# One weight load for two neighbouring ring slots, instead of one load each, in a one-core diffusion trunk

## The chip, the core and the metric

The kernel runs on one core of a Trainium2 chip. The metric is device time in microseconds (us); lower is better. A core has TensorE (PE; its weight loads are shown as PEld), VectorE (DVE), ScalarE (ACT), GpSimd (POOL) and SyncE (SP). SP and POOL each issue DMAs on a queue of their own, and both queues run on the same 16 DMA engines.

## The reference, cut to what matters

Two layers over 256 latent tokens of width 2048; layer 0 also reads 256 context tokens. All is float32. Layer 0 mixes tokens by differential attention, layer 1 by a gated short convolution, and each is followed by a gated ConvFFN of inner width 5632:

```python
for i in range(DEPTH):                        # 2 layers
    sh1, sc1, g1, sh2, sc2, g2 = adaln(c, w_ada[i], b_ada[i])   # silu(c) @ w_ada + b_ada
    hl = modulate(rmsnorm(xl), sh1, sc1)
    if i % 2 == 0: yl, _ = diff_attn_mixer(hl, hc, w_qkv, w_o, ...)   # K and V of the context too
    else:          yl = short_conv_mixer(hl, w_in, conv_w, w_out)     # (gb * conv3(gc * xv)) @ w_out
    xl = xl + g1 * yl
    xl = xl + g2 * conv_ffn(modulate(rmsnorm(xl), sh2, sc2), w_up[i], conv_w[i], w_down[i])
return rmsnorm(xl, final_gain)
```

The large products are `h @ w` with w of qkv 2048x6144, o 2048x2048, in 2048x6144, out 2048x2048, and twice up 2048x11264 and down 5632x2048.

## The kernel before

**Units and phases.** All weights but those of `w_ada` come through a ring of four slots. A *unit* is what one slot holds: 4 tiles of 128 rows by 256 columns of a weight, 512 KB (`KU = 4`, `SLAB = 256`, `RING = 4`). A *slab* is 256 output columns; it takes four units, one in each slot, and in the down phases twelve, of which the last four hold 3 tiles (384 KB). There are 800 units in this order: V (32 units of another shape), K, Q and O (32 each), up0 (176), dn0 (96), sin (96, the product with `w_in`), so (32), up1 (176), dn1 (96). Unit n sits in slot n mod 4; `4 * quad + slot` in the code is n.

**Three rings, one behind the other.** Each unit passes through `raw` (float32, filled by DMA), `w_hi` (ACT's rounded copy) and `w_lo` (DVE's difference raw - w_hi), each with four slots:

- SP, `load` (the DMA is L376): waits until DVE has made `w_lo` of unit n-4, which frees the raw slot, and issues the DMA of unit n.
- ACT, `hi` (L591): waits for the DMA (`raw_full[slot]`) and until PE has used unit n-4 (`w_used`), and copies.
- DVE, `lo` (L1070): waits for `hi` of the unit, and subtracts.
- PE, `unit` (L1770 and L1772): waits for `lo` of the unit, and issues for each tile and each half of the slab a matmul of 512 columns with `w_hi` (high and low halves of the activations) and one of 256 columns with `w_lo`. In K the same is done for the context too (L1760, L1761). V has lines of its own (L1687 to L1689), and its DMA is L385.

**Order of the work.** Every engine's order is written out by hand. ACT and DVE begin each unit with its `hi` or `lo` and then do, in that order, what is due at this point: the slab before is copied from PSUM (L634, L1210), convolved, gated or added to the residual, and DVE multiplies chunks of `w_ada` by the condition (L1131, and L1187 for broad chunks), which gives the modulation vectors. These chunks are loaded by POOL's queue into rings of their own (`ada_ring`, two slots of 512 KB; `broad_ring`, two of 1 MB). PE takes up the next slab but one only when the slab's PSUM banks have been read (`acc_read`).

**Between phases** that begin with a norm, PE waits for the sum of squares of the last slab and for the modulated activations.

In the O phase the first eight units (`O_FIRST`) are taken from two slabs in turn, between parts of the attention.

Of the kernel before, what the change touches and what calls it, by code (L numbers as in the profile page):

```python
# [7 lines left out]
ACT = mybir.ActivationFunctionType  # L8
# [8 lines left out]
QK = 2048  # L17
D_FF = 5632
# [6 lines left out]
SLAB = 256  # L25
RING = 4
KU = 4
# [10 lines left out]
V_UNITS = 32  # L38
UNITS, SLABS = {}, {}
# [73 lines left out]
def down_tiles(k):  # L113

    return (4 * k, 4) if k < 8 else (32 + 3 * (k - 8), 3)


def program(nc, x, c, ctx_in, c_ctx, w_ada, b_ada, w_qkv, w_o, lq1, lk1, lq2, lk2, subln, w_in, conv_in,
            w_out, w_up, conv_ffn, w_down, final_gain, ident_in, rope_cos_in, rope_sin_in, out):
    tiles = lambda w: w.rearrange("(t p) n -> p t n", p=P)  # L120
    qkv_w, o_w, in_w, out_w = tiles(w_qkv[0]), tiles(w_o[0]), tiles(w_in[0]), tiles(w_out[0])
# [6 lines left out]
    with ExitStack() as scope:  # L128
# [13 lines left out]
        def at(name, shape, dt, offset):  # L142
            return nc.alloc_sbuf_tensor_at(name, shape, dt, offset=offset)
# [15 lines left out]
        res = at("res", [P, KT, T], F32, at_res)  # L159

        raw = at("raw", [P, RING, KU, SLAB], F32, at_raw)
        w_hi = at("w_hi", [P, RING, KU, SLAB], F32R, at_hi)
        w_lo = at("w_lo", [P, RING, KU, SLAB], F32R, at_lo)

# [56 lines left out]
        def first_chunk(b, q):  # L221

            if b == 0:
                return first_c[:, q + 2, :, :] if q in (4, 5) else first_x[:, q, :, :]
            return first_x[:, 4 + q, :, :] if q < 2 else first_c[:, q - 2, :, :]

        def sums_slot(n):
            return first_x[:, 6 + n % 4, :, :] if n % 4 < 2 else first_c[:, 4 + n % 4, :, :]
# [47 lines left out]
        raw_full = [sem(f"raw_full{n}") for n in range(RING)]  # L276
        hi_made, lo_made, w_used = sem("hi_made"), sem("lo_made"), sem("w_used")
# [29 lines left out]
        def wait(eng, s, n):  # L307

            if isinstance(n, int) and n <= 0:
                return  # L310
            eng.wait_ge(s, n)
# [40 lines left out]
        @block.sync  # L352
        def _(sp):


            def ada_rows(q, col):
                return ada_w[0][:, 2 * q:2 * q + 2, col:col + ADA_COLS]

            def to_multiply(n):

                g, q = n // 8 + 1, n % 8

                wait(sp, start_used, n - 3)
                sp.dma_start(start_ring[:, n % 4, :, :], ada_rows(q, SH1 * P + g * ADA_COLS)).then_inc(start_full[n % 4], 16)

            def to_sum(n):

                g, q = n // 8 + 1, n % 8

                sp.wait_ge(start_step, 32 if n < 4 else 32 + 4 * (n - 3))  # L370
                sp.dma_start(sums_slot(n), ada_rows(q, SC1 * P + g * ADA_COLS)).then_inc(sums_full[n % 4], 16)

            def load(quad, slot, w, tile, n_tiles, col):

                wait(sp, lo_made, 4 * quad + slot - 3)
                sp.dma_start(raw[:, slot, 0:n_tiles, :], w[:, tile:tile + n_tiles, bass.ds(col, SLAB)]  # L376
                             ).then_inc(raw_full[slot], 16)

            wide = raw[:, :, :, :].rearrange("p r (t h) n -> p r t (h n)", h=2)

            def v_unit(n):
                g, slab, k = n // 8, n % 8 // 2, n % 2

                wait(sp, lo_made, n - 3)
                sp.dma_start(wide[:, n % 4, :, :], qkv_w[:, 4 * g + 2 * k:4 * g + 2 * k + 2, slab * VSLAB + 2 * QK:(slab + 1) * VSLAB + 2 * QK]  # L385
                             ).then_inc(raw_full[n % 4], 16)

            for q in range(8):
                for b, col in enumerate((SC1, SH1)):
                    sp.dma_start(first_chunk(b, q), ada_rows(q, col * P)).then_inc(first_full[8 * b + q], 16)  # L390
                if q == 0:
                    sp.dma_start(x_tok[:, :, :], x_rows).then_inc(x_loaded, 16)
                if q == 2:
                    sp.dma_start(ctx_tok[:, :, :], ctx_rows).then_inc(ctx_loaded, 16)
                if q == 5:
                    v_unit(0)
            for n in range(1, 4):
                v_unit(n)
            for n in range(24):
                to_sum(n)  # L400
                to_multiply(n)
                v_unit(n + 4)
            for n in range(28, V_UNITS):
                v_unit(n)
            with sp.Fori(0, 8) as s:
                for k in range(4):
                    load(s + UNITS["k"] // 4, k, qkv_w, 4 * k, 4, s * SLAB + QK)

            def plain(phase, w, base):
                with sp.Fori(0, 8) as s:  # L410
                    for k in range(4):
                        load(s + UNITS[phase] // 4, k, w, 4 * k, 4, s * SLAB + base)

            def up(phase, w):
                with sp.Fori(0, FT // 2) as j:
                    for h in range(2):
                        for k in range(4):
                            load(2 * j + (UNITS[phase] // 4 + h), k, w, 4 * k, 4, j * SLAB + h * D_FF)

            def down(phase, w):  # L420
                with sp.Fori(0, 8) as s:
                    for k in range(12):
                        tile, n = down_tiles(k)
                        load(3 * s + (UNITS[phase] // 4 + k // 4), k % 4, w, tile, n, s * SLAB)

            plain("q", qkv_w, 0)
            for n, (s, k) in enumerate(O_FIRST):
                load(UNITS["o"] // 4 + n // 4, n % 4, o_w, 4 * k, 4, s * SLAB)
            with sp.Fori(2, 8) as s:
                for k in range(4):  # L430
                    load(s + UNITS["o"] // 4, k, o_w, 4 * k, 4, s * SLAB)
            up("up0", up_w[0])
            down("dn0", dn_w[0])

            with sp.Fori(1, 9) as n:
                for h, first in ((0, D), (1, 2 * D), (2, 0)):
                    for k in range(4):
                        load(3 * n + (UNITS["sin"] // 4 + h - 3), k, in_w, 4 * k, 4, n * SLAB + (first - SLAB))
            plain("so", out_w, 0)
            up("up1", up_w[1])  # L440
            down("dn1", dn_w[1])

            for t in range(2):
                sp.wait_ge(fin_scaled[t], 1)
                sp.dma_start(out_rows[:, t, :], out_tok[:, t, :]).then_inc(fin_stored, 16)
            sp.wait_ge(fin_stored, 32)
# [90 lines left out]
        def _(se):  # L537
# [47 lines left out]

            def hi(quad, slot, n_tiles=KU):

                se.wait_ge(raw_full[slot], 16 * quad + 16)

                wait(se, w_used, 4 * quad + slot - 3)  # L590
                nc.scalar.activation(w_hi[:, slot, 0:n_tiles, :], raw[:, slot, 0:n_tiles, :], ACT.Copy).then_inc(hi_made, 1)  # L591

            keep_tokens(0, xn_l, xn_kept)
            keep_tokens(1, xn_c, ctx_kept)
            copy_rows(0)
            hi(0, 0)
            modulate(0, 0)
            hi(0, 1)
            modulate(0, 1)
            se.wait_ge(vecs_turned, 1)  # L600
# [9 lines left out]
            for g in range(4):  # L610
                for u in range(8):
                    n = 8 * g + u
                    if n + 2 < V_UNITS:
                        hi((n + 2) // 4, (n + 2) % 4)
                    if 2 <= n < 10:
                        keep_v(n - 2)
                    if u == 6 and g < 3:
                        copy_rows(g + 1)
                    if n == 3:
                        se.wait_ge(lam_summed, 1)  # L620
                        nc.scalar.activation(lam_exp[:, :], ps[:, 7, 16:18], ACT.Exp).then_inc(lam_exped, 1)
                    if u == 7 and g < 3:
                        if g == 1:
                            se.wait_ge(ada_reduced, ADA_WIDE[0])
                        modulate(g + 1, 0)
                        modulate(g + 1, 1)
# [354 lines left out]
        def _(ve):  # L981
# [85 lines left out]
            def lo(quad, slot, n_tiles=KU):  # L1067

                ve.wait_ge(hi_made, 4 * quad + (slot + 1))
                nc.vector.tensor_tensor(w_lo[:, slot, 0:n_tiles, :], raw[:, slot, 0:n_tiles, :],  # L1070
                                        w_hi[:, slot, 0:n_tiles, :], ALU.subtract).then_inc(lo_made, 1)

            def add_mods(g):
# [16 lines left out]
            ve.wait_ge(plus_one, 2)  # L1090
            add_mods(0)
            lo(0, 0)
            low_h(0, 0)
            lo(0, 1)
            low_h(0, 1)

# [42 lines left out]
            for g in range(4):  # L1139
                for u in range(8):  # L1140
                    n = 8 * g + u
# [953 lines left out]
```

## Time and profile before

| | |
|---|---|
| Time, three runs | 2691.7 us median (2685.12 to 2699.36) |
| Profiled execution | 2694.76 us, its span 2693.1 us |
| PE busy | 2603.8 us, 97% of the span |
| DVE, ACT, POOL busy | 2002.1, 1290.7, 198.5 us |
| Mean granted TensorE clock | 0.981 |
| DMA | 623.51 MB, mean 232 GB/s; SP's queue 50.8% and POOL's 19.9% of the 16 engines' span |

PE is busy for nearly all of the span, and the chain that ended last runs through PE for 90% of it. The other engines have idle time on average, but DVE has little of it from up0 to so. A DMA's time to landing is counted from its issue to the last of its semaphore's updates.

### The profile page before, as it was taken

The numbers are of one execution on the slowest core, as the hardware profiler recorded it, in microseconds if no ns is written. First come the engines' busy times: TensorE is split into PE (matmuls) and PEld (weight loads), VectorE is DVE, ScalarE is ACT, GpSimd is POOL, SyncE is SP. The second block draws the span as 40 slices with busy tenths as digits, with TensorE's granted clock in tenths as the row PEclk, the third lists the DMA queues.
The fourth block names the chain that finished last, engine by engine and source line by source line (L and its number), as shares of the span: only waits on it lengthen the run. The fifth ranks groups of instructions, "written<-read, shape, count | busy, mean of one in ns | idle before, by whom it ended". The sixth has DMA issues, their size and how long they took to land.

```text
span 2693.1 us, 39832 instructions
## 1 busy us (share of the span) xinstructions
PE 2603.8 (97%) x14306; PEld 2196.5 (82%) x14306; DVE 2002.1 (74%) x2571; ACT 1290.7 (48%) x1730; POOL 198.5 (7%) x301
## 2 busy tenths in 40 slices
PE   6999999998989999999999899999899999999998
PEld 3666788876878888888888788888788888888887
DVE  5776988676778887997778678978788876665543
ACT  4322233467655554555444444445555545554443
POOL 1000222000000000110111001101000000000000
PEclk8999999999999999999999899999999999999999
DMA  8765988333657786886999679978678865565553
GB/s 309 267 238 166 303 280 275 116 106 129 204 179 250 261 264 217 284 288 210 288 296 296 224 253 319 340 229 274 201 243 271 264 185 186 184 186 186 182 183 129
DMA packets 464924, 623.51 MB, mean 232 GB/s; under 512 B 18772, under 2 KB 404214, under 8 KB 457616
## 3 DMA queue, kind: packets, MB, share of 16 engines
q1 hardware_dynamic: 424256, 450.94, 50.8%
q0 software_dynamic: 40208, 170.51, 19.9%
q8 instruction: 95, 1.56, 0.2%
q14 instruction: 45, 0.37, 0.0%
q10 hardware_dynamic: 320, 0.13, 0.0%
HBM read 619.41 MB, written 2.10 MB: 231 GB/s over the span
## 4 chain that ended last, share of the span: by engine, by line
PE 90%; DVE 4%; ACT 3%; issue 3%; DMA 1%; SPq 0%; ACTq 0%; POOL 0%; DVEq 0%
PE ps L1770 48%; PE ps L1772 24%; PE ps L1760 4%; PE ps L1761 2%; PE ps L1631 2%; PE ps L1687 2%; PE ps L1688 2%; PE ps L1689 2%; PE ps L1699 1%; DMA first_c<-in_w_ada_dram 1%; ACT w_hi L591 1%; DVE w_lo L1070 1%; ACT rot L640 1%; DVE s_max L1350 0%; PE ps L1706 0%
## 5 line engine op out<-in xcount | busy, mean ns | idle before, releaser
L1770 PE MATMUL ps<-xs,w_hi 128*128 128x512 f32 x3840 | 1364.6, 400 | 21.8 <-issue 21.8
L1070 DVE TENSOR_TENSOR w_lo<-raw,w_hi 128x1024 fp32r<-128x1024 f32 (+1 forms) x800 | 957.6, 1201 | 383.7 <-ACT w_hi L591 382.4
L591 ACT ACTIVATE w_hi<-raw 128x1024 fp32r<-128x1024 f32 (+1 forms) x800 | 831.7, 1041 | 856.0 <-PE ps L1772 555.8
L1772 PE MATMUL ps<-xs,w_lo 128*128 128x256 f32 x3840 | 1077.1, 280 | 0.0
L1770 PEld LDWEIGHTS ps<-xs,w_hi 128*128 128x128 f32 x3840 | 726.4, 189 | 199.3 <-issue 26.1
L1772 PEld LDWEIGHTS ps<-xs,w_lo 128*128 128x128 f32 x3840 | 729.3, 190 | 3.3 <-issue 3.1
L1770 PE MATMUL ps<-act,w_hi 128*128 128x512 f32 x1408 | 494.6, 397 | 0.0
L1772 PE MATMUL ps<-act,w_lo 128*128 128x256 f32 x1408 | 392.8, 279 | 0.0
L1770 PEld LDWEIGHTS ps<-act,w_hi 128*128 128x128 f32 x1408 | 264.3, 188 | 63.1
L1772 PEld LDWEIGHTS ps<-act,w_lo 128*128 128x128 f32 x1408 | 265.2, 188 | 0.0
L634 ACT ACTIVATE y<-ps 128x512 f32<-128x512 f32 x128 | 76.7, 599 | 206.7 <-PE ps L1772 206.7
L1210 DVE TENSOR_TENSOR y<-y,ps 128x512 f32<-128x512 f32 x128 | 87.9, 687 | 99.1 <-ACT y L634 99.0
L502 POOL DMA_DIRECT2D ada_ring<-in_w_ada_dram x128 | 91.2, 713 | 783.9 <-DVE ada_sum L1131 557.9
L1131 DVE SCALAR_TENSOR_TENSOR ada_sum<-ada_ring,cond,ada_sum 128x512 f32<-128x512 f32 x185 | 138.7, 750 | 8.1 <-DMA ada_ring<-in_w_ada_dram 4.0
L1187 DVE SCALAR_TENSOR_TENSOR broad_sum<-broad_ring,cond,broad_sum 128x2048 f32<-128x2048 f32 x45 | 105.6, 2346 | 0.0
L1770 PE MATMUL ps<-heads_out,w_hi 128*128 128x512 f32 x256 | 93.6, 409 | 1.0 <-DVE y L1210 0.8
L1760 PE MATMUL ps<-cs,w_hi 128*128 128x512 f32 x256 | 91.8, 399 | 2.0 <-DVE v_rows L1105 2.0
L1760 PE MATMUL ps<-xs,w_hi 128*128 128x512 f32 x256 | 91.1, 397 | 1.8 <-DVE v_rows L1105 1.8
L1770 PE MATMUL ps<-z,w_hi 128*128 128x512 f32 x256 | 89.8, 396 | 0.0
L1772 PE MATMUL ps<-heads_out,w_lo 128*128 128x256 f32 x256 | 72.0, 281 | 0.0
L1761 PE MATMUL ps<-cs,w_lo 128*128 128x256 f32 x256 | 71.6, 280 | 0.0
L1772 PE MATMUL ps<-z,w_lo 128*128 128x256 f32 x256 | 71.3, 279 | 0.0
(219 smaller groups left out, 2609.6 us busy)
## 6 DMA issues: line engine op xcount, KB each, us to landing
raw<-in_ffn_w_up_dram SPq DMA_DIRECT2D x352, 512.0 KB, 4.4
ada_ring<-in_w_ada_dram POOLq DMA_DIRECT2D x168, 512.0 KB, 5.5
raw<-in_ffn_w_down_dram SPq DMA_DIRECT2D x128, 512.0 KB, 3.4
raw<-in_attn_w_qkv_dram SPq DMA_DIRECT2D x96, 512.0 KB, 5.5
broad_ring<-in_w_ada_dram POOLq DMA_DIRECT2D x48, 1024.0 KB, 6.2
raw<-in_sconv_w_in_dram SPq DMA_DIRECT2D x96, 512.0 KB, 6.0
raw<-in_ffn_w_down_dram SPq DMA_DIRECT2D x64, 384.0 KB, 3.1
ada_ring_kv<-in_w_ada_dram POOLq DMA_DIRECT2D x40, 512.0 KB, 6.2
```

Of the source, the lines that this page charges most:

```text
L502: pool.dma_start(ada_slot(q % ADA_SLOTS), ada_w[layer][:, 2 * q:2 * q + 2, col:col + ADA_COLS]).then_inc(ada_full[q % ADA_SLOTS], 16)
L591: nc.scalar.activation(w_hi[:, slot, 0:n_tiles, :], raw[:, slot, 0:n_tiles, :], ACT.Copy).then_inc(hi_made, 1)
L634: nc.scalar.activation(dst, ps[:, bank:bank + 2, 0:T], ACT.Copy).then_inc(a_copied, 1)
L1070: nc.vector.tensor_tensor(w_lo[:, slot, 0:n_tiles, :], raw[:, slot, 0:n_tiles, :], w_hi[:, slot, 0:n_tiles, :], ALU.subtract).then_inc(lo_ ...
L1131: nc.vector.scalar_tensor_tensor(out=out, in0=w, scalar=scalar, in1=out, op0=ALU.mult, op1=ALU.add).then_inc(ada_step, 1)
L1187: nc.vector.scalar_tensor_tensor(out=broad_sum[:, :], in0=w, scalar=scalar, in1=broad_sum[:, :], op0=ALU.mult, op1=ALU.add).then_inc(broad ...
L1210: nc.vector.tensor_tensor(dst, dst, ps[:, bank:bank + 2, T:2 * T], ALU.add).then_inc(acc_read, 1)
L1631: last = mm(ps[0:2, 6, :], cond[:, :, 2 * q + t], rows[:, t, :], start=(q == 0 and t == 0), stop=(q == 7 and t == 1))
L1760: mm(ps[:, bank + m, :], w_hi[:, k, t, cols], src[:, 4 * k + t, :], start=(k == 0 and t == 0), stop=False)
L1761: last = mm(ps[:, bank + m, 0:T], w_lo[:, k, t, cols], src[:, 4 * k + t, 0:T], start=False, stop=(k == 3 and t == 3))
L1770: mm(ps[:, bank + m, :], w_hi[:, slot, t, cols], src[:, tile + t, :], start=(is_first and t == 0), stop=False)
L1772: last = mm(ps[:, bank + m, 0:T], w_lo[:, slot, t, cols], src[:, tile + t, 0:T], start=False, stop=(is_last and t == n_tiles - 1))
```

## The change

From K on, one DMA brings the weights of two units into two neighbouring slots: 8 tiles, 1 MB; in the down phases 6 tiles, 768 KB, for two units of 3 tiles. `load_two` waits for `lo_made >= 4 * quad + slot - 2`, that is until DVE has made `w_lo` of both units that were in the two slots, and signals the even slot's semaphore alone. ACT waits for the DMA only before the even unit; for the odd unit it then needs none, except in V and in the eight units of `O_FIRST`, which still come one by one. The second of two short units now lies right behind the three tiles of the first, and `raw_unit` gives both engines the place. `hi`, `lo` and PE's work stay one per unit, and their order is unchanged.

```diff
+        raw_tiles = raw[:, :, :, :].rearrange("p r t n -> p (r t) n")
+        raw_unit = lambda slot, n: raw_tiles[:, KU * (slot // 2 * 2) + n * (slot % 2):KU * (slot // 2 * 2) + n * (slot % 2) + n, :]
...
+            def load_two(quad, slot, w, tile, n_tiles, col):
+
+                wait(sp, lo_made, 4 * quad + slot - 2)
+                sp.dma_start(raw_tiles[:, KU * slot:KU * slot + 2 * n_tiles, :], w[:, tile:tile + 2 * n_tiles, bass.ds(col, SLAB)]
+                             ).then_inc(raw_full[slot], 16)
...
                 with sp.Fori(0, 8) as s:
-                    for k in range(4):
-                        load(s + UNITS[phase] // 4, k, w, 4 * k, 4, s * SLAB + base)
+                    for k in (0, 2):
+                        load_two(s + UNITS[phase] // 4, k, w, 4 * k, 4, s * SLAB + base)
...
-                    for k in range(12):
+                    for k in range(0, 12, 2):
                         tile, n = down_tiles(k)
-                        load(3 * s + (UNITS[phase] // 4 + k // 4), k % 4, w, tile, n, s * SLAB)
+                        load_two(3 * s + (UNITS[phase] // 4 + k // 4), k % 4, w, tile, n, s * SLAB)
...
             def hi(quad, slot, n_tiles=KU):
 
-                se.wait_ge(raw_full[slot], 16 * quad + 16)
+                single = V_UNITS // 4
+                if slot % 2 == 0 or isinstance(quad, int) and quad < single:
+                    se.wait_ge(raw_full[slot], 16 * quad + 16)
+                elif isinstance(quad, int) and 0 <= quad - UNITS["o"] // 4 < 2:
+                    se.wait_ge(raw_full[slot], 16 * (single + quad - UNITS["o"] // 4) + 16)
 
                 wait(se, w_used, 4 * quad + slot - 3)
-                nc.scalar.activation(w_hi[:, slot, 0:n_tiles, :], raw[:, slot, 0:n_tiles, :], ACT.Copy).then_inc(hi_made, 1)
+                nc.scalar.activation(w_hi[:, slot, 0:n_tiles, :], raw_unit(slot, n_tiles), ACT.Copy).then_inc(hi_made, 1)
...
             def lo(quad, slot, n_tiles=KU):
 
                 ve.wait_ge(hi_made, 4 * quad + (slot + 1))
-                nc.vector.tensor_tensor(w_lo[:, slot, 0:n_tiles, :], raw[:, slot, 0:n_tiles, :],
+                nc.vector.tensor_tensor(w_lo[:, slot, 0:n_tiles, :], raw_unit(slot, n_tiles),
                                         w_hi[:, slot, 0:n_tiles, :], ALU.subtract).then_inc(lo_made, 1)
```

The loops of K, O from its third slab on, up and sin are changed in the same way as `plain` above.

## Rows read from the trace of the kernel before

**Rows 1.** The page: engines' busy time, and the chain that ended last.
```profile
PE 2603.8 (97%) x14306; PEld 2196.5 (82%) x14306; DVE 2002.1 (74%) x2571; ACT 1290.7 (48%) x1730; POOL 198.5 (7%) x301
...
PE 90%; DVE 4%; ACT 3%; issue 3%; DMA 1%; SPq 0%; ACTq 0%; POOL 0%; DVEq 0%
```

**Rows 2.** Waits of PE from 300 us on: us in total, times, longest.
```profile
PE ps L1770 <- issue: 21.8, 3, 8.0
PE ps L1825 <- DVE o_rows L1372: 8.3, 5, 2.8
PE ps L1783 <- ACT part_c L669: 7.1, 3, 2.7
...
PE ps L1770 <- DVE w_lo L1070: 0.2, 1, 0.2
```

**Rows 3.** Windows by phase: K, up0's second part, dn0, up1's second part, dn1.
```profile
core 0: us, PE busy (x) PEld busy (x) DVE busy (x) ACT busy (x) POOL busy (x), PEclk, DMA share, GB/s
...
271.00:500.00 229.00, 225.18 (x1276) 195.88 (x1275) 191.20 (x254) 70.40 (x88) 52.08 (x74) 0.99 0.80 264
...
1000.00:1265.00 265.00, 265.00 (x1530) 232.35 (x1529) 225.15 (x301) 139.00 (x183) 24.77 (x35) 0.99 0.80 253
1265.00:1515.00 250.00, 250.00 (x1459) 219.14 (x1458) 194.39 (x240) 112.39 (x133) 32.80 (x46) 1.00 0.89 282
...
2145.00:2409.00 264.00, 264.00 (x1504) 229.51 (x1503) 184.95 (x234) 140.03 (x184) 0.53 (x1) 0.99 0.61 188
2409.00:2670.00 261.00, 261.00 (x1489) 226.78 (x1488) 133.02 (x141) 118.20 (x143) 0.00 (x0) 1.00 0.55 177
```

**Rows 4.** Windows inside sin: all work, then work on w_lo alone.
```profile
1591.00:1772.00 181.00, 181.00 (x1041) 158.35 (x1040) 163.58 (x176) 83.47 (x96) 22.37 (x34) 1.00 0.94 320
...
1591.00:1772.00 181.00, 143.46 (x513) 96.64 (x512) 77.19 (x64) 1.00 0.94 320
```

**Rows 5.** Groups of instructions on the whole span (the page): hi and lo.
```profile
L1070 DVE TENSOR_TENSOR w_lo<-raw,w_hi 128x1024 fp32r<-128x1024 f32 (+1 forms) x800 | 957.6, 1201 | 383.7 <-ACT w_hi L591 382.4
L591 ACT ACTIVATE w_hi<-raw 128x1024 fp32r<-128x1024 f32 (+1 forms) x800 | 831.7, 1041 | 856.0 <-PE ps L1772 555.8
```

**Rows 6.** Tile raw in 1599 to 1602 us: issues, first and last start, landing.
```profile
L1070 DVE TENSOR_TENSOR w_lo<-raw,w_hi x3: 1221/1221/1225, 1597.8 to 1600.2; 128x1024 fp32r<-128x1024 f32 x3
...
L376 SPq DMA_DIRECT2D raw<-in_sconv_w_in_dram x3: 373/373/373, 1599.2 to 1601.6; - x3
...
DMA to landing us min/median/max: 6.1/6.3/6.4
```

**Rows 7.** DMA issues by window: up0 first part, up0 second, dn0, sin, up1, dn1.
```profile
raw<-in_ffn_w_up_dram SPq DMA_DIRECT2D x85, 512.0 KB, 4.6
broad_ring<-in_w_ada_dram POOLq DMA_DIRECT2D x15, 1024.0 KB, 5.5
...
raw<-in_ffn_w_up_dram SPq DMA_DIRECT2D x91, 512.0 KB, 4.7
...
raw<-in_ffn_w_down_dram SPq DMA_DIRECT2D x64, 512.0 KB, 5.2
ada_ring<-in_w_ada_dram POOLq DMA_DIRECT2D x46, 512.0 KB, 5.4
...
raw<-in_sconv_w_in_dram SPq DMA_DIRECT2D x96, 512.0 KB, 6.0
broad_ring<-in_w_ada_dram POOLq DMA_DIRECT2D x16, 1024.0 KB, 7.2
...
raw<-in_ffn_w_up_dram SPq DMA_DIRECT2D x176, 512.0 KB, 3.8
...
raw<-in_ffn_w_down_dram SPq DMA_DIRECT2D x64, 512.0 KB, 3.3
raw<-in_ffn_w_down_dram SPq DMA_DIRECT2D x32, 384.0 KB, 2.9
```

**Rows 8.** Waits of ACT inside sin, 1515 to 1805 us.
```profile
ACT w_hi L591 <- PE ps L1772: 51.8, 37, 2.9
ACT w_hi L591 <- DMA raw<-in_sconv_w_in_dram: 45.1, 30, 4.7
```

**Rows 9.** Chain that ended last, at the end of O.
```profile
763.05 3.40 DVE w_lo L1070 x3
766.46 0.61 DVE y L1210
767.09 0.89 DVE res L1246 x2
768.01 0.64 ACT part_c L669
768.69 1.13 PE ps L1783 x4
769.82 6.68 issue
```

**Rows 10.** Windows of 4 us at the norm between dn0 and sin.
```profile
1526.00:1530.00 4.00, 4.00 (x25) 3.48 (x25) 2.45 (x2) 1.96 (x3) 0.00 (x0) 1.00 0.72 209
1530.00:1534.00 4.00, 2.17 (x12) 1.58 (x10) 3.16 (x5) 2.26 (x4) 1.10 (x2) 1.00 0.83 226
1534.00:1538.00 4.00, 1.93 (x4) 1.02 (x4) 2.42 (x3) 1.10 (x3) 0.00 (x0) 0.57 0.97 392
```

More of the change, by code:

```diff
@@ L405, in _ @@
             with sp.Fori(0, 8) as s:
-                for k in range(4):
-                    load(s + UNITS["k"] // 4, k, qkv_w, 4 * k, 4, s * SLAB + QK)
+                for k in (0, 2):
+                    load_two(s + UNITS["k"] // 4, k, qkv_w, 4 * k, 4, s * SLAB + QK)
             def plain(phase, w, base):
                 with sp.Fori(0, 8) as s:
-                    for k in range(4):
-                        load(s + UNITS[phase] // 4, k, w, 4 * k, 4, s * SLAB + base)
+                    for k in (0, 2):
+                        load_two(s + UNITS[phase] // 4, k, w, 4 * k, 4, s * SLAB + base)
             def up(phase, w):
@@ L416, in up @@
                     for h in range(2):
-                        for k in range(4):
-                            load(2 * j + (UNITS[phase] // 4 + h), k, w, 4 * k, 4, j * SLAB + h * D_FF)
+                        for k in (0, 2):
+                            load_two(2 * j + (UNITS[phase] // 4 + h), k, w, 4 * k, 4, j * SLAB + h * D_FF)
             def down(phase, w):
                 with sp.Fori(0, 8) as s:
-                    for k in range(12):
+                    for k in range(0, 12, 2):
                         tile, n = down_tiles(k)
-                        load(3 * s + (UNITS[phase] // 4 + k // 4), k % 4, w, tile, n, s * SLAB)
+                        load_two(3 * s + (UNITS[phase] // 4 + k // 4), k % 4, w, tile, n, s * SLAB)
             plain("q", qkv_w, 0)
@@ L429, in _ @@
             with sp.Fori(2, 8) as s:
-                for k in range(4):
-                    load(s + UNITS["o"] // 4, k, o_w, 4 * k, 4, s * SLAB)
+                for k in (0, 2):
+                    load_two(s + UNITS["o"] // 4, k, o_w, 4 * k, 4, s * SLAB)
             up("up0", up_w[0])
@@ L436, in _ @@
                 for h, first in ((0, D), (1, 2 * D), (2, 0)):
-                    for k in range(4):
-                        load(3 * n + (UNITS["sin"] // 4 + h - 3), k, in_w, 4 * k, 4, n * SLAB + (first - SLAB))
+                    for k in (0, 2):
+                        load_two(3 * n + (UNITS["sin"] // 4 + h - 3), k, in_w, 4 * k, 4, n * SLAB + (first - SLAB))
             plain("so", out_w, 0)
```

## The prediction

> **What bounds the kernel now.** I read the page first: PE is busy for 2603.8 of 2693.1 us and carries 90% of the chain that ended last [rows 1]. Then PE's waits after the start: in 2390 us PE waits for `w_lo` once, for 0.2 us; the rest are pauses at the norms (issue, ACT part_c) and inside attention [rows 2]. So no load holds PE back today, and a change to the loads can win nearly nothing. It can only lose, if landings come so late that the cover is used up. The windows tell where the cover is thin: in sin the DMA engines are busy 94% of the time at 320 GB/s [rows 4], in dn0 89%, in up0 80%, in dn1 only 55% [rows 3].
>
> **What is removed.** Of 768 loads on SP from K on, 760 become 380. SP's queue spends its time in waits for `w_lo`, so fewer issues save nothing. ACT loses a semaphore wait before most odd units: nothing. Matmuls, `hi` and `lo` are the same in number and size. The bytes are the same too. Sum of these: 0, and the cover is PE itself.
>
> **What is added: an even unit is asked for one unit later, and lands with twice the bytes.** Before, unit n was issued when `lo` of n-4 was done. Now n and n+1 are issued when `lo` of n-3 is done. The odd unit loses nothing in its issue, the even one loses one unit's time, 2.8 us. What decides is whether the round of a slot pair still fits in four units of PE time. The round is: issue, landing, hi of n (1.06 us), lo of n (1.22), what DVE does between two lo's, lo of n+1 (1.22), and 0.2 from its end to the next issue [rows 5, 6]: the last of three lo's begins at 1600.2, ends at 1601.4, and the DMA goes at 1601.6.
>
> *sin, 1591 to 1772 us.* 64 lo's in 181 us are 2.83 us a unit, so a round may take 11.3 us. DVE is busy 163.58 us, 2.56 per unit, of which 1.34 is not lo [rows 4]. The work of the round without the landing is 1.06 + 1.22 + 1.34 + 1.22 + 0.2 = 5.0. This leaves 6.3 us for the landing of 1 MB. The 512 KB loads of today take 6.0 at the median [rows 7], and ACT already waits for them 30 times, 45.1 us in all [rows 8]; PE doesn't feel it, because four slots with a request each keep two or more loads in the queue. How long 1 MB takes on this queue no row shows. From below: the 1 MB loads of POOL's queue in the same phase land in 7.2 [rows 7]. From above: a first load issued at 1599.2 and a second 1.2 us behind it, landing 6.3 after its issue, are down after 7.5 [rows 6]; and if the second half simply adds its bytes, at 0.4 us for 128 KB (3.3 against 2.9 for 512 and 384 KB in dn1, [rows 7]), it is 6.0 + 1.6 = 7.6, or up to 7.9 from the 6.3 of [rows 6]. I take 7.5: the pair of requests is the nearest row. The round then lacks 7.5 - 6.3 = 1.2 us, and a late lo makes the next request late, so the lack adds up from slab to slab: 16 slabs x 1.2 = 19 us. Against it stands the cover once: hi of n can start when PE ends n-4, PE wants the unit three units later, 8.5 us, less 2.3 for hi and lo and some 1.3 for work ahead of them: 5 us. sin costs 19 - 5 = 14 us. The first and last slabs of sin are left out, since PE's pause at the norm refills the rings.
>
> *dn0.* 97 lo's in 250 us (96 units and one of the next phase) are 2.58 us a unit, a round 10.3 us. DVE is busy 2.00 per unit, 0.78 beside lo [rows 3]. The rest of the round is 1.06 + 1.22 + 0.78 + 1.22 + 0.2 = 4.5, so 5.8 is left. Landing: below, the 5.4 of POOL's 512 KB; above, 5.2 + 1.6 = 6.8 [rows 7]. I take 6.3, as the two halves overlapped in part before. It lacks 0.5, times 24 rounds is 12, less 5 of cover: 7 us.
>
> *up0, second part.* 92 units in 265 us are 2.88, a round 11.5; DVE 225.15 us is 2.45 per unit, 1.23 beside lo; the rest is 4.9, so 6.6 is left [rows 3]. Landing 4.7 + 1.6 = 6.3 at most, and 5.5 by the 1 MB loads in the first part [rows 7]: it fits on average, and I put 2 us for the slabs in which the chunks of `w_ada` are crowded.
>
> *The others.* K has 42 units in 229 us, 5.45 each, so a round has 21.8 us: hidden. up1's second part: 2.84 a unit (93 in 264 us), DVE 1.99; left 11.4 - 4.5 = 6.9 against 3.8 + 1.6 = 5.4: hidden. dn1: 2.64 a unit (99 in 261 us), DVE 1.34; left 10.5 - 3.8 = 6.7 against 3.3 + 1.6 = 4.9: hidden by 1.8 us, the safest place [rows 3, 7].
>
> *Ends of phases.* At the end of O three lo's of the next phase stand on the critical chain ahead of the last slab's y [rows 9]. DVE takes them in order, so if one of the loads is late, the norm is. Four such places, 0.5 us each: 2 us.
>
> Sum: 14 + 7 + 2 + 2 = 25 us. The profiled execution took 2694.8 us (span 2693.1 and 1.7 around it), 3.1 above the median of the runs; it would become 2720, and the median 2691.7 + 25 = 2717.
>
> What hangs behind a late hi: ACT's copy of the slab before (L634), and DVE's read of PSUM behind lo; PE waits for that with `acc_read` two slabs on, so it has four units of cover and comes later than the wait on `lo_made`.
>
> By the Trainium skill ("DMA: Bandwidth & Descriptors", Anatomy of one DMA) a DMA costs about 2.0 us plus its bytes at 436 GB/s, which is an estimate of 3.2 us for 512 KB and 4.4 for 1 MB, and the same page's rules for kernel authors want 1 MB or more per DMA. The quiet dn1 agrees with 3.3 for 512 KB [rows 7]; sin, with 6.0, does not. By that formula every round fits, and the sum would be 0 instead of 25.
>
> **The rivals.** *All hidden.* If 1 MB as one request lands in 6.3 or less in sin, because the second half rode beside the first before as well, no round is short, and the time is that of before: 2692, or up to 2705 if only sin overruns a little. For it: PE waits for `w_lo` 0.2 us in all. Against it: sin's room is what 512 KB takes now. *A deeper loss.* If 1 MB takes 7.9 in sin and 6.8 in dn0, it is 16 x 1.6 - 5 = 21 and 24 x 1.0 - 5 = 19, some 6 for up0's crowded slabs, 4 at the ends: 50 us, 2742; if pauses of PE are long enough to bring the granted clock down, as PE's pause at the norm ahead of sin does (0.57 of full, near the 1.2 GHz level, [rows 10]), up to 2755. *Faster.* The one mechanism is less load on the DMA engines and thus earlier landings at ends of phases and in attention, where w_lo stands in DVE's order ahead of what PE waits for. It decides if a 1 MB load landed no later than its even unit does today, 2.8 us plus 6.0 after today's issue. It could shorten the pauses of [rows 2], 8.3 + 7.1 us, at most to nothing: 2692 - 15 = 2677. Against it: these pauses end with DVE and ACT arithmetic, none with a load.
>
> **How the numbers follow.** Forecast (a loss of 13 to 40 us) 0.53; deeper loss 0.12; all hidden, within 13 us, 0.30; faster 0.05. Half a per cent, 13.5 us, is what a measurement can tell here, the three runs being 14 us apart. The likeliest case gives 2717, its own range 2705 to 2732. The whole range reaches down to 2687, since the hidden case centres on 2692, and up to 2752 for the deeper loss. Faster 0.05, same 0.30, slower 0.65.
>
> **What would show it.** Right: SP has some 420 issues of raw instead of 800, 1 MB landing in about 7.5 us in sin, 6.3 in dn0, 5 in dn1; ACT waits for raw at most even units in sin and dn0, far over 45 us; PE waits for w_lo L1070 some 20 us, nearly all in sin and dn0; K, dn1 and up1's second part take as long as before. Wrong: a landing near 6 us in sin with no wait of PE (all hidden), PE waits on w_lo in up0 and up1 as well (deeper), or a DMA share in sin that falls without the phase getting longer. The weakest term is the 1 MB landing under load: 0.5 us of it is worth 8 us in sin and 12 in dn0.

## The result, and the profile after

The changed kernel takes 2753.1 us at the median of 4 runs (2747.9 to 2758.7), the kernel before 2694.1 us beside it; the ratio is 1.023, with a 95% interval of 1.020 to 1.026. It is 59 us slower. The forecast was 2717 and slower, with a range that ended at 2752: the sign and the mechanism held, the size (25 us) was less than half of what came.

The page of the profile after, with the engines, the chain that ended last and three groups of instructions, of which the last two answer to [rows 5] (lines have moved by 12: `hi` is L603, `lo` L1082, PE's unit L1782 and L1784, `load_two` L384):

```profile
PE 2632.1 (95%) x14306; PEld 2203.4 (80%) x14306; DVE 1995.9 (72%) x2571; ACT 1275.7 (46%) x1730; POOL 198.4 (7%) x301
...
PE 60%; DMA 16%; DVE 14%; ACT 5%; issue 5%; SPq 0%; ACTq 0%; POOL 0%; DVEq 0%; POOLq 0%
...
L1782 PE MATMUL ps<-xs,w_hi 128*128 128x512 f32 x3840 | 1378.3, 403 | 47.9 <-DVE w_lo L1082 26.1
L1082 DVE TENSOR_TENSOR w_lo<-raw,w_hi 128x1024 fp32r<-128x1024 f32 (+1 forms) x800 | 956.1, 1201 | 514.5 <-ACT w_hi L603 513.0
L603 ACT ACTIVATE w_hi<-raw 128x1024 fp32r<-128x1024 f32 (+1 forms) x800 | 821.9, 1038 | 991.9 <-PE ps L1784 248.5
```

The chain that ended last no longer stays on PE: 35% of it now runs through DMA, DVE and ACT, against 8% in [rows 1]. PE is still 95% busy. DVE waits 513 us for `hi`, against 382 in [rows 5], and `hi`'s largest wait for PE is down from 556 to 248 us. Its waits for the DMA in the up, down and sin phases are up from 61 to 458 us in all.

PE's waits from 300 us on, as in [rows 2]:

```profile
PE ps L1782 <- DVE w_lo L1082: 34.9, 38, 2.1
PE ps L1782 <- issue: 21.8, 3, 8.0
PE ps L1795 <- ACT part_c L681: 8.8, 3, 3.3
```

The wait for `w_lo` went from 0.2 us to 34.9; the waits at the norms (`part_c`) grew by 1.7 us and the others changed by less. The rest of the 59 us is no wait by this view. PE's weight loads, which go ahead of the matmuls, show more of it: the page has PEld idle ahead of L1782 for 239.6 us and ahead of the same line with `act` for 75.7. Before they were 199.3 and 63.1, so it is 53 us more.

The stretches inside up0, dn0, sin, up1 and in dn1; all work, then sin's row for w_lo alone (they answer to [rows 3, 4]):

```profile
918.00:1013.00 95.00, 90.61 (x510) 77.50 (x508) 72.47 (x86) 46.92 (x64) 3.19 (x6) 1.00 0.74 251
1337.00:1515.00 178.00, 171.93 (x979) 147.95 (x979) 126.64 (x157) 67.66 (x83) 24.01 (x34) 1.00 0.83 271
1619.00:1823.00 204.00, 189.47 (x1045) 160.97 (x1044) 162.83 (x175) 80.90 (x97) 21.66 (x33) 0.98 0.84 285
2116.00:2250.00 134.00, 129.25 (x726) 110.91 (x725) 106.33 (x124) 68.39 (x92) 3.72 (x7) 1.00 0.70 237
2489.00:2740.00 251.00, 251.00 (x1434) 218.07 (x1433) 122.60 (x128) 109.43 (x132) 0.00 (x0) 1.00 0.55 173
...
1619.00:1823.00 204.00, 145.06 (x514) 98.30 (x514) 77.12 (x64) 0.98 0.84 285
```

In sin PE is busy 93% instead of 100%, and the DMA engines 84% instead of 94%: with two requests in four slots, there is no load of `raw` between its issue and its landing for 8% of the stretch, against 0.5% before. The 64 lo's that took 181 us now take 204, so a round of four units takes 12.75 us instead of 11.3. dn1 is untouched.

The granted clock in the stretch of sin is 0.98 instead of 1.00. One place shows how a wait and the clock go together: PE waits 2.1 us for `w_lo` in the first of these two windows, and in the second the granted clock is 0.57, near the 1.2 GHz level, and PE starts 16 matmuls where 25 is usual.

```profile
1691.00:1695.00 4.00, 1.92 (x12) 1.45 (x11) 3.88 (x5) 0.00 (x0) 0.71 (x1) 1.00 0.85 268
1695.00:1699.00 4.00, 4.00 (x16) 3.37 (x15) 2.07 (x3) 2.48 (x3) 0.00 (x0) 0.57 0.80 249
```

By the clock records of the traces the lower level was granted for 102.5 and 95.3 us in the two profiles of the kernel before and for 111.6 and 110.2 us in those of the changed one. That is 12 us more, and at half the clock it is worth 6 us of the 59 at most.

Issues and landings of `raw` after, to be held against [rows 7] (the line of the down phases mixes dn0, with a median of 6.3, and dn1, with 5.0), and inside sin:

```profile
raw<-in_ffn_w_up_dram SPq DMA_DIRECT2D x176, 1024.0 KB, 5.0
...
raw<-in_ffn_w_down_dram SPq DMA_DIRECT2D x64, 1024.0 KB, 5.1
...
raw<-in_sconv_w_in_dram SPq DMA_DIRECT2D x48, 1024.0 KB, 6.4
```

```profile
  DMA raw<-in_sconv_w_in_dram: 108.1, 31
...
DMA to landing us min/median/max: 4.9/6.5/10.6
```

One MB lands sooner than forecast (6.5 us at the median in this stretch, where 7.5 was taken), and ACT still waits for it 31 times, before nearly every even unit, 108 us in all. One whole round can be read in the chain that ended last, 1690 to 1704 us:

```profile
1688.49 7.33 DMA raw<-in_sconv_w_in_dram
1695.82 0.02 issue
1695.84 1.06 ACT w_hi L603
1696.91 0.02 issue
1696.93 0.52 DVE w_lo L1082
1697.45 0.62 issue
1698.07 0.68 DVE part_a L1222
1698.75 0.67 DVE ada_sum L1143
1699.43 0.03 issue
1699.45 0.75 DVE ada_sum L1143
1700.20 1.15 DVE w_lo L1082
...
1701.50 8.24 DMA raw<-in_sconv_w_in_dram
```

The load of a pair is issued at 1688.49, the next into the same two slots at 1701.50: 13.0 us for four units of PE time, which are 11.3. It has the steps of the forecast's round, in its order: landing 7.33, hi 1.06, lo, DVE's other work (part_a, two chunks of `w_ada`), lo, issue. No PE work is in it.

Where the time went, by the moment at which PE signals that it has used the last unit of each phase (us; two profiles of each kernel, the second pair taken later):

| phase | before | after | after less before, mean |
|---|---|---|---|
| V, K, Q, O | 765.2, 761.6 | 768.1, 766.2 | +4 |
| up0 | 516.7, 521.3 | 526.1, 528.8 | +8 |
| dn0 | 249.5, 252.4 | 263.7, 262.3 | +12 |
| sin | 291.6, 291.7 | 315.9, 311.5 | +22 |
| so | 91.3, 91.3 | 91.3, 90.5 | 0 |
| up1 | 511.4, 512.0 | 523.6, 524.3 | +12 |
| dn1 | 251.8, 251.0 | 251.8, 251.2 | 0 |

Of the 4 us in the first row 2 are in V, which the change leaves alone, and two profiles of one kernel differ by 2 to 4 us there.

### The profile page after: what moved, and what is told of

Same layout as the page of the kernel before. It is cut to its first block, busy times and chain, and to the rows that moved or that the text cites. A ratio compares the mean times of both kernels' runs of the same rounds, so it can differ in the third digit from the quotient of the medians.

```text
span 2757.0 us, 38017 instructions
## 1 busy us (share of the span) xinstructions
PE 2632.1 (95%) x14306; PEld 2203.4 (80%) x14306; DVE 1995.9 (72%) x2571; ACT 1275.7 (46%) x1730; POOL 198.4 (7%) x301
## 4 chain that ended last, share of the span: by engine, by line
PE 60%; DMA 16%; DVE 14%; ACT 5%; issue 5%; SPq 0%; ACTq 0%; POOL 0%; DVEq 0%; POOLq 0%
PE ps L1782 29%; PE ps L1784 15%; DMA raw<-in_ffn_w_up_dram 6%; DVE w_lo L1082 6%; PE ps L1772 4%; DMA raw<-in_sconv_w_in_dram 4%; DMA raw<-in_ffn_w_down_dram 4%; ACT w_hi L603 3%; DVE broad_sum L1199 2%; PE ps L1773 2%; PE ps L1643 2%; PE ps L1699 2%; PE ps L1700 2%; PE ps L1701 2%; DMA raw<-in_attn_w_o_dram 1%
## 5 line engine op out<-in xcount | busy, mean ns | idle before, releaser
L1782 PE MATMUL ps<-xs,w_hi 128*128 128x512 f32 x3840 | 1378.3, 403 | 47.9 <-DVE w_lo L1082 26.1
L1082 DVE TENSOR_TENSOR w_lo<-raw,w_hi 128x1024 fp32r<-128x1024 f32 (+1 forms) x800 | 956.1, 1201 | 514.5 <-ACT w_hi L603 513.0
L603 ACT ACTIVATE w_hi<-raw 128x1024 fp32r<-128x1024 f32 (+1 forms) x800 | 821.9, 1038 | 991.9 <-PE ps L1784 248.5
L1784 PE MATMUL ps<-xs,w_lo 128*128 128x256 f32 x3840 | 1081.8, 282 | 0.0
L1782 PEld LDWEIGHTS ps<-xs,w_hi 128*128 128x128 f32 x3840 | 727.1, 189 | 239.6 <-issue 50.0
L1784 PEld LDWEIGHTS ps<-xs,w_lo 128*128 128x128 f32 x3840 | 730.8, 190 | 3.3 <-issue 3.1
L1782 PE MATMUL ps<-act,w_hi 128*128 128x512 f32 x1408 | 499.4, 399 | 8.1 <-DVE w_lo L1082 8.0
L1784 PE MATMUL ps<-act,w_lo 128*128 128x256 f32 x1408 | 394.9, 280 | 0.0
L1782 PEld LDWEIGHTS ps<-act,w_hi 128*128 128x128 f32 x1408 | 264.4, 188 | 75.7 <-DVE w_lo L1082 7.8
L1784 PEld LDWEIGHTS ps<-act,w_lo 128*128 128x128 f32 x1408 | 265.9, 189 | 0.0
L1782 PE MATMUL ps<-heads_out,w_hi 128*128 128x512 f32 x256 | 93.2, 407 | 1.9 <-DVE y L1222 0.8
L1782 PE MATMUL ps<-z,w_hi 128*128 128x512 f32 x256 | 89.8, 396 | 0.0
L1784 PE MATMUL ps<-heads_out,w_lo 128*128 128x256 f32 x256 | 71.7, 280 | 0.0
L516 POOL DMA_DIRECT2D broad_ring<-in_w_ada_dram x48 | 25.9, 541 | 631.9 <-DVE broad_sum L1199 419.1
L1784 PE MATMUL ps<-z,w_lo 128*128 128x256 f32 x256 | 71.3, 279 | 0.0
## 6 DMA issues: line engine op xcount, KB each, us to landing
ada_ring<-in_w_ada_dram POOLq DMA_DIRECT2D x168, 512.0 KB, 5.0
ada_ring_kv<-in_w_ada_dram POOLq DMA_DIRECT2D x40, 512.0 KB, 6.1
```

The costliest lines, as they stand in the source:

```text
L603: nc.scalar.activation(w_hi[:, slot, 0:n_tiles, :], raw_unit(slot, n_tiles), ACT.Copy).then_inc(hi_made, 1)
L1082: nc.vector.tensor_tensor(w_lo[:, slot, 0:n_tiles, :], raw_unit(slot, n_tiles), w_hi[:, slot, 0:n_tiles, :], ALU.subtract).then_inc(lo_mad ...
L1782: mm(ps[:, bank + m, :], w_hi[:, slot, t, cols], src[:, tile + t, :], start=(is_first and t == 0), stop=False)
L1784: last = mm(ps[:, bank + m, 0:T], w_lo[:, slot, t, cols], src[:, tile + t, 0:T], start=False, stop=(is_last and t == n_tiles - 1))
```

## The experiments

Two theories go into them. *The round*: time is lost where issue, landing, hi, lo, DVE's other work, lo and the next issue take longer than four units of PE, and only there. *Its rivals*: the later request by itself; the size of a request by itself; DMA contention alone or DVE alone.

**Late requests, but singly.** The load of each unit stays 512 KB with a semaphore of its own, and only its wait is the new one:

```diff
-                wait(sp, lo_made, 4 * quad + slot - 3)
+                wait(sp, lo_made, 4 * quad + (slot // 2 * 2 if pairs else slot - 1) - 2)
```

> One DMA of 512 KB per unit as in the kernel before, each with its own semaphore, but both of a pair are issued only when lo of unit n-3 is done, as in the changed kernel. Theory of the round (the loss comes of the chain issue, landing of 1 MB, hi, lo, DVE's work, lo, issue being longer than four units of PE time): the even unit lands some 1.5 us ahead of the odd one, its hi and lo run meanwhile, and the round falls to landing of both (7 us in sin) + 2.3 + 0.2 = 9.5 us, under 11.3: the time is that of before, 2694, at most 10 us more. Rival, the late request (what costs is that the even unit is asked for 2.8 us later, and four requests in the queue become two): as the changed kernel, some 2750.

Measured: 2697.8 us, ratio 1.0031 (1.0005 to 1.0057). PE waits for w_lo 3.8 us, 3.6 of them in sin, which is 6 us longer; the other phases are within 3. In sin the 512 KB loads land in 5.8 at the median. So asking late costs 4 us of the 59 (1 to 15 by the interval). In sin the even unit is down 1.4 us ahead of the odd one in the mean, so its hi is done while the odd unit is still on its way, which is what the single load of 1 MB takes away.

The same trace answers a rival: that one request of 1 MB is slower than two of 512 KB. From the first issue until both units of a pair are down it takes 6.9 us in sin, 6.2 in dn0, 6.0 in up0 and 5.5 in up1 (means). The loads of 1 MB in the changed kernel take 6.6, 6.2, 5.9 and 5.4.

**Old requests, but ACT waits for both.**

```diff
                 se.wait_ge(raw_full[slot], 16 * quad + 16)
+                if slot % 2 == 0 and not (isinstance(quad, int) and (quad < V_UNITS // 4 or 0 <= quad - UNITS["o"] // 4 < 2)):
+                    se.wait_ge(raw_full[slot + 1], 16 * quad + 16)
```

(The test on `quad` leaves out V and the eight units of `O_FIRST`.)

> The loads of the kernel before, singly and at their old times, but ACT waits before an even unit for the odd unit's load too. Theory of the round: the chain is landing of 512 KB, then the same hi and lo's: sin 6.3 + 3.0 + 2.6 + 0.2 = 12.1 us against 11.3, 0.8 us too long, 20 rounds less 3 of cover: about 13 us; dn0 5.1 + 4.8 = 9.9 against 10.3 and up0, up1 4.8 + 5.7 = 10.5 against 11.3: nothing. Together 2700 to 2715. Rival, the late request: nothing is asked for later, so 2694. Rival, the size of a request (1 MB requests hold up POOL's loads): 2694 as well.

Measured: 2712.0, ratio 1.0073 (1.0047 to 1.010), 19 us. PE waits for w_lo 12.9 us, of which 11.8 are in sin; sin is 16 us longer. The forecast of the round, 13 us and all in sin, is right in place and nearly in size. Neither half of the change makes the loss by itself, 4 and 19 us against 59: it takes the late request and the common landing in one round. No run has both halves with single requests; that the joining of the requests as such adds nothing rests on the landings under the experiment before.

**DVE's share.** The broad chunks' sums are narrowed from 2048 to 64 columns (from the second chunk of each vector on), in the kernel before and in the changed one; the modulation of the other columns is left out:

```diff
-nc.vector.scalar_tensor_tensor(out=broad_sum[:, :], in0=w, scalar=scalar, in1=broad_sum[:, :],
+nc.vector.scalar_tensor_tensor(out=broad_sum[:, 0:64], in0=w[:, 0:64], scalar=scalar, in1=broad_sum[:, 0:64],
```

> The kernel before, with DVE's sums over the broad chunks of w_ada narrowed from 2048 to 64 columns after each first chunk (2.35 us become some 0.1, 45 times; the loads stay; the other columns' modulation is left out). PE doesn't wait for DVE outside the norms, so every theory expects 2694 within 5 us. It is the base for the next.

> The changed kernel with the same narrowing, DMAs unchanged. Theory of the round: a broad chunk of 2.35 us stands between two lo's in two rounds of five to ten in the first parts of up0, sin and up1, and delays lo of the even unit; without it the round falls under 11.3 us in up0 and up1, whose losses (9 and 12 us) go, and sin's falls from 24 to about 10; dn0's 14 stays: 2715 to 2725. Rival, the DMA queue alone (landing sets the loss, DVE has room): 2750 as the changed kernel, since all landings are as long.

Measured: 2696.0 on the kernel before (ratio 1.0013, 0.9985 to 1.0041), and 2729.3 on the changed one (1.0135, 1.0074 to 1.0196; four runs, three near 2729 and one at 2715.7), where 2715 to 2725 was expected. PE's waits after the narrowing, from 300 us on:

```profile
PE ps L1782 <- DVE w_lo L1082: 14.6, 14, 2.4
```

34.9 became 14.6 us: none is left in up0 and up1, 7.5 in sin and 6.7 in dn0, which has no broad chunks. up0 and up1 are 4 and 5 us longer than in the first profile of before, with no wait for w_lo in them; this is within what PE's two paces do (last section). sin is 11 and dn0 13 us longer, near the 10 and 14 that were expected. DVE work that costs nothing in the kernel before costs some 24 us here, with the same DMAs: contention alone is out.

**The landing's share.** POOL loads a quarter of `w_ada`'s bytes from O on (of the broad chunks too, the first two of each vector apart). DVE's work is kept, on what lies in the rest of the slots, so the modulation of those columns is left out:

```diff
-pool.dma_start(ada_slot(q % ADA_SLOTS), ada_w[layer][:, 2 * q:2 * q + 2, col:col + ADA_COLS]
+pool.dma_start(ada_slot(q % ADA_SLOTS)[:, :, 0:P], ada_w[layer][:, 2 * q:2 * q + 2, col:col + P]
```

> The changed kernel, but from the O phase on POOL loads a quarter of each chunk of w_ada (128 of 512 columns, 512 of 2048 for all but the first two broad chunks); DVE's work stays as it is, on what lay in the rest of the rings (the modulation of those columns is left out). It separates the landing from DVE's work. Theory of the round: landing in sin falls from 6.9 to about 5.4 us, the round to 11.4 against 11.3; in dn0 it is 5.2 + 4.6 + 0.2 = 10.0 against 10.3, in up0 and up1 5.2 + 5.6 = 10.8 against 11.3. Nearly all of the loss goes: 2694 to 2705. Rival, 1 MB requests are slow by themselves on SP's queue: 2750 stays. Rival, DVE alone sets it: 2750 too.

Measured: 2698.0, ratio 1.0026 (1.0002 to 1.0051). 1 MB in sin lands in 5.1 at the median instead of 6.4:

```profile
raw<-in_sconv_w_in_dram SPq DMA_DIRECT2D x48, 1024.0 KB, 5.1
```

PE waits for w_lo 2.9 us, all in sin, and sin takes 299.7 us in this profile, 8 more than before. The 1 MB loads are all there, and 54 of the 59 us are gone: they don't cost the 59 by their size alone, nor does DVE's work alone. With both cuts:

> The changed kernel with both cuts: a quarter of w_ada's bytes, and the sums over broad chunks narrowed to 64 columns. Theory of the round: every phase has room, sin 5.4 + 5.0 + 0.2 = 10.6 against 11.3; 2690 to 2698, no PE wait for w_lo. Any rival in which late requests or their size cost by themselves expects some of the 59 us to stay.

Measured: 2697.6, ratio 1.0023 (0.9999 to 1.0048), no wait of PE for w_lo, sin 290.4 us. With all the 1 MB loads in place nothing that can be told from noise is left of the loss.

**By place.** The pairs in dn0 and sin alone (the diff shows dn0; sin has the pairs of the changed kernel):

```diff
-                    for k in range(12):
+                    for k in range(0, 12, 2 if phase == "dn0" else 1):
                         tile, n = down_tiles(k)
-                        load(3 * s + (UNITS[phase] // 4 + k // 4), k % 4, w, tile, n, s * SLAB)
+                        (load_two if phase == "dn0" else load)(3 * s + (UNITS[phase] // 4 + k // 4), k % 4, w, tile, n, s * SLAB)
```

> The kernel before, with the loads in pairs in dn0 and sin alone. Theory of the round: each phase loses by itself what it lost in the changed kernel, since the pauses at the norms refill the rings: dn0 +14, sin +24, all others 0, 2732. Rival, lateness carried on from up0 makes much of dn0's loss: dn0 +5, 2720. Rival, the smaller number of requests from K on matters as such: up0 and up1 as in the kernel before, dn0 and sin less than half.

Measured: 2724.1, ratio 1.0129 (1.0083 to 1.0175): 31 us where 38 was expected. PE waits for w_lo 19.4 us, none outside the two phases; dn0 is 11 and sin 17 us longer than in the first profile of before. So dn0 loses without pairs in up0 ahead of it, as much as with them (10 to 14 us), and little or nothing is handed on. sin lost less here than in the two profiles of the changed kernel (17 us for 20 and 24); one profile doesn't tell why.

**More room instead of less time.** In sin alone, eight raw slots for four, in SBUF space that is free then; the loads stay 1 MB:

```diff
+        raw_b = at("raw_b", [P, RING, KU, SLAB], F32, at_u + 32 * KB)
...
+                            wait(sp, lo_made, 4 * quad + (slot - 6))
+                        dst = (raw_tiles, raw_b_tiles)[g % 2]
+                        sp.dma_start(dst[:, KU * slot:KU * slot + 2 * KU, :], src
```

The wait was `4 * quad + slot - 2`; `g` counts the quads, so every other one goes to the new slots.

> The changed kernel, with eight raw slots in place of four in sin alone (16 KB more a partition, in space that is free in that phase; every other slab goes to the new slots; w_hi and w_lo keep four). 1 MB loads stay, in the same number. Theory of the round: the round of a slot pair may now take eight units, 22.6 us, against 12.8, so sin takes 292 us as in the kernel before, PE waits for w_lo in sin fall to nothing, landings stay at 6.5 to 8 us, and the whole is 2753 - 24 = 2729. Rival, 1 MB requests hurt by their burst on the DMA engines (POOL's chunks late, DVE late): sin stays over 305 us.

Measured: 2726.5, ratio 1.0142 (1.0101 to 1.0183), against 1.023 for the changed kernel. Inside sin (all work), and the landings into the new slots alone:

```profile
1600.00:1800.00 200.00, 200.00 (x1161) 175.09 (x1161) 180.84 (x196) 92.68 (x108) 24.26 (x37) 1.00 0.91 316
```

```profile
DMA to landing us min/median/max: 5.0/7.4/12.5
```

PE is busy all the time again, the DMA engines 91% at 316 GB/s, and sin takes 287.5 us, with landings that are longer than in the changed kernel: 7.4 us into the new slots and 7.9 into the old ones, for 6.4. PE waits for w_lo nowhere in sin. So in sin long landings do no harm if the ring holds another pair. It isn't a better kernel: only sin is mended. With all phases mended I would expect the time of the kernel before, in which PE waits 0.2 us for `w_lo`, but no run tried it.

**The two kernels once more**, for a second profile of each (in the table above).

> The kernel before, unchanged, for a second profile of it. In the profiles so far the time of one unit on PE, where nothing waits, is 2.77 us in some stretches and 2.82 in others at the same granted clock. If that is bound to a place in the program, the same stretches show it again; if it changes from run to run, up0 and up1 differ from the first profile by up to 9 us, and this much of the differences by phase isn't the change's.

> The changed kernel, unchanged, for a second profile. Theory of the round: waits of PE for w_lo again 35 us, in the same phases (sin most, dn0, then the first parts of up0 and up1), dn1 and so none; sin 18 to 26 us over the kernel before, dn0 9 to 15.

Measured, one run each: 2698.4 and 2752.5. PE waits for w_lo 37.2 us in the second profile after, with sin 20 us over before and dn0 10 to 13, as expected. The pace of PE is not bound to a place, see the last section.

## Why the prediction was wrong

*PE bound, nothing to win.* Right. No run was faster, and the fewer requests, the wait that ACT lost and SP's shorter loops gave nothing back.

*The round of a slot pair.* Right as a mechanism: it can be read whole in the chain, and what it says of place mostly came true (dn1, so and K lose nothing, sin most). Its sum was wrong: 25 us for 59. The step that failed is the size of its terms, and most of all that up0 and up1 stood in it with 2 us and nothing. They lost 8 and 12, dn0 12 for 7, sin 22 for 14. The terms:

- *up0 and up1*, 2 us and nothing. This was the worst step. I put the second part of each through the sum and left out the first part of both, which has the broad chunks of 2.35 us; and I took DVE's work as a mean. In the mean the first parts fit by my own rule. But a broad chunk comes every 15 us, in every fifth or sixth unit, and the round that holds it is too long: in 918 to 1013 us of the profile after, hi to the end of lo is 3.3 us, not 2.28. Narrowing the chunks ends every wait of PE for w_lo there, which shows it.
- *Landing in sin*, 7.5 taken, 6.5 at the median and 6.7 in the mean of the stretch. In dn0 6.3 was taken; the mean over the phase is 6.2. I had called these the weakest terms, and they held or erred toward a greater loss.
- *The rest of the round*, 5.0 us taken in sin. It failed. In the same stretch the mean from the start of hi to the end of its lo is 2.9 us, not 2.28, as DVE is often still at other work when hi is done; from there to the end of the second lo it is 2.6. With 0.1 ahead of hi and 0.2 to the issue that is 5.8, and 6.7 + 5.8 = 12.5, within 0.3 of the 12.75 of the windows. I had counted DVE's other work once per pair, between the two lo's; it also stands ahead of the first. A round lacked 1.4 us, not 1.2; that these are so near is luck, since the landing was taken 0.8 too long and the rest 0.8 too short.
- *The cover of 5 us.* In sin this did more than the lack of a round. The 64 units of the forecast's stretch (units 16 to 80 of sin) took 181.1 and 181.2 us in the two profiles before and 203.6 and 200.0 after: they lost 22.5 and 18.8 us, which is 16 times 1.4 and 1.2, with no cover to take off. The time from the end of a unit's lo until PE is done with the unit ahead of it was 3.7 and 3.1 us there before, not 5, and is 1.2 after, and the first rounds of the phase, which the sum left out, had used up the cover. In dn0 it was 5.2 and 5.3 us before, about as taken.
- *dn0's round*, 10.8 us taken, was 11.1: landing 6.2, 0.3 to the start of hi, 2.2 to the end of its lo, 2.2 to the end of the second, 0.2 to the issue. PE's time for it was 10.4 to 10.5 us (249.5 and 252.4 us for 24 rounds), not 10.3. It lacked 0.6 to 0.7, and 24 times that less 5 is 9 to 12; it lost 12.
- *Ends of phases*, 2 us: the waits at the norms grew by 1.7 us (8.8 for 7.1 in `part_c`), as said.

*The rivals.* "All hidden" fell with the first profile. "A deeper loss" came, with the time it named (2742, up to 2755), and so did its sign, waits for w_lo in up0 and up1 (6.5 and 5.0 us). But it came by another road: this rival expected landings of 7.9 us in sin, and they were 6.5. The clock, which it named for the last 13 us, had a small part: 6 us at most. "Faster" had nothing for it.

*The Trainium skill.* "DMA: Bandwidth & Descriptors" (Anatomy of one DMA) gives its formula for the path of GpSimd; for 1 MB it is an estimate of 4.4 us. These loads go by SP's queue: in dn1, where POOL's queue brings nothing, they take 5.0 at the median, and in sin 6.5. So it comes within 0.6 us in dn1 and falls short by 2 in sin, and the measured landings decide.

The same page's rules for kernel authors ask for 1 MB or more per DMA where the most bandwidth is wanted. Here the loads of 1 MB brought no more (mean 226 GB/s for 232) and the kernel was 2.3% slower, because the ring did not grow with the request: in sin, with eight slots, the loss was gone.

What PE's signals add: where nothing waits, eight long units with no other work of PE among them take 22.2 or 22.6 us. In the kernel before, units 40 to 88 of up0 and of up1 keep to that. In the changed kernel they take 7.5 and 8.7 us more than six times 22.6 in up0 (the two profiles), and 6.6 and 10.6 in up1. That is about what the rounds cost there; the rest of the differences between phases is PE's pace and what happens at their ends. Why the rounds of up1 cost 4 us less in one profile than in the other stays open.

## What to carry to other kernels

Before two transfers into a ring are joined, write down the round of a slot: issue, landing, every instruction that must free it, in the order of its engine with what stands ahead of each, and the next issue; then compare it with the time in which the bound engine uses up the ring, stretch by stretch and for the crowded rounds, not for the mean. Joining adds twice: the first slot is asked for later, and nothing may start until the last byte is there. If an engine off the critical path has no idle time in a stretch, its work counts in that round, though it costs nothing today. A request of double size wants a ring of double length; in sin this took the whole loss away.

## What the runs showed of the hardware

PE has two paces at the same granted clock. Where it doesn't wait, a unit of 16 matmuls takes 2.77 us in some stretches and 2.82 in others (2.08 and 2.12 for the short ones), and which it is changes inside a phase and from run to run of the same kernel. By PE's signals eight units of the first part of up1 take 22.2 us in the first profile of the kernel before and 22.6 in the second, and in the second part it is the other way round. Two profiles of the kernel before, 1110 to 1240 us, work on w_lo alone, clock 1.00 in both (first the first profile, then the second):

```profile
1110.00:1240.00 130.00, 101.70 (x368) 68.91 (x368) 56.45 (x47) 1.00 0.86 273
```

```profile
1110.00:1240.00 130.00, 101.23 (x361) 68.13 (x361) 54.41 (x46) 1.00 0.86 269
```

It is 368 against 361 matmuls in the same 130 us, 1.9%, and 22.6 against 22.2 us is 1.8%. This makes a phase like up0 5 us longer or shorter (516.7 and 521.3) and dn0 3 us, so that a difference of that size between two profiles of one phase says nothing. No experiment here tells where it comes from.
